# A two-block transformer kernel on one core: x also loaded by columns, bias rows from the host, another order at the start, and a shifted ring

## The chip, the core and the metric

The kernel runs on one core of a Trainium2 chip. A core has five engines that run their own instruction streams: TensorE (PE, matrix products), VectorE (DVE), ScalarE (ACT), GpSimd (POOL) and SyncE (SP), and 16 DMA engines that all queues share. SP and POOL issue the transfers here. The streams are tied together by semaphores alone: an instruction waits until a count is reached, another adds to it. The metric is the time of one execution on the device, in microseconds (us), median of the runs.

## What is computed

x has 256 rows (tokens) of 1024 numbers, all in 32-bit floats. The first block makes queries, keys and values of 24 heads in three groups with relative-position biases:

```
h = _rmsnorm(x, norm_gain[l])
z = h @ w_in[l]
a_in, a_gate, q, k, v, b_gp, g_logits = jnp.split(z, splits, axis=-1)
y_a = (_multiscale_pool(a_in, w_pool[l], pool_scale[l]) * jax.nn.silu(a_gate)) @ w_proj_a[l]
att = _dilated_attention(q.reshape(shp), k.reshape(shp), v.reshape(shp), rel_bias)
...
x = x + merged @ w_out[l]
```

where `_rmsnorm` is x times one root per row, times a gain per column. Because the root is one number per row, it can be applied behind the product as well: (x * gain) @ w, each row then times its root. The second block is a convolution mixer, an attention with a window (bias from `rel_bias_2`), and after each of them an expert layer with retrieval: each token picks 128 of 16,384 experts (8 heads, 16 each) and reads two rows of 1024 numbers of each:

```
u = jnp.take(u_tab, ic, axis=0)
h = jnp.einsum("cd,ced->ce", xc, u)
a = gc.astype(xc.dtype) * jax.nn.gelu(h, approximate=False)
return jnp.einsum("ce,ced->cd", a, jnp.take(v_tab, ic, axis=0))
```

## The kernel before

Everything is written out by hand in one function, one stream per engine; there is no scheduler, and the order in the code is the order on the engine. The tokens stand in two tiles of 128 (`TILES`), the 1024 columns in eight chunks of 128 (`KC`).

**The start.** SP issues x tile 0, the identity (part of `const`), x tile 1, `pf` (gains per column), the query weights of the first pair of heads in three parts by group (`first_landed`), the key weights, the table `bucket`, the rest of `const`, the value weights, `final_gain`, and then the weights of the further pairs as `wbuf` comes free (`load_heads`). TensorE does 16 products of ones with ones (L1008), turns the two tiles of x with the identity (16 transposes, `turn`, L959), does six more products of ones (L1015), and waits for ACT and DVE, which copy the turned chunks from PSUM, times the gain, to `raw` (`turned_out`, L698 and L1564). `raw` is x by columns with the gain and without the root. The first queries come of `raw` (`first_queries`, L1034). Meanwhile ACT sums the squares of each row (`norm`, L674) and DVE makes the roots of them (`root_of`) and a diagonal of them (`row_diag`, L1530); after the second group of queries TensorE spreads the roots over the partitions with two products (L1039). DVE copies them to `root_row`, makes `hT` = `raw` times roots (L1591), and scales the queries while it copies them to `q1` (L1594). Then it makes `hT4`, an arrangement of `hT` for the values (L1602, L1603).

TensorE goes on with `bias_rows`: four products of `rb` (the bias tables) with `bucket`, a table of zeros and ones (L1106 to L1110). ACT copies the result, POOL writes it to DRAM (L613, L614), waits for that, and reads it back in six loads with short strided rows, `hank0` (L618, twice) and `hank4` (L623, four times). DVE copies these reversed to `bias1` (L1608, L1611). The keys (`project`, L1025) come of `hT`, so TensorE waits for `hT_scaled` before them. ACT copies them to `k1` (L722). Then come the scores (L1061, L1067), the values (L1050), and the next pair of heads. There are four pairs (`PAIRS1`).

**The expert layers.** Two loops of 256 gathers. POOL issues one gather for each expert slot (L651, the last three of a layer in halves): 128 rows of 2048 numbers, 8 KB to each partition, into one of nine places of `ring`. DVE takes a dot product with the first half (L1906), ACT makes the weight and a diagonal of it (L834, L839, L844), TensorE adds the second half, weighted, in PSUM (L1373) and frees the place (`ring_free`). Between the products TensorE does those of later queries and keys. Their weights come to `wbuf` (L537) and to `w4`, a part of `arena` (L587, L590).

**Where things lie.** A tensor starts where the one before it ends, in the order of the `sb(...)` lines; `ring` is a part of `arena`:

```
sinks = sb("sinks", [P, HEADS2])
...
small = sb("small", [P, 64])
arena = sb("arena", [P, 32128])
...
ring = at(16, RING, 2 * D)
w4 = at(20640, KC, 512)
```

In the built program `arena` starts at byte 99,968 of each partition, so the first place of the ring at 100,032 (192 above a multiple of 512), and `w4` at 182,528, a multiple of 256; `wbuf` starts at 16,512, 128 above a multiple of 256.

Of the kernel before, what the change touches and what calls it, by code (L numbers as in the profile page):

```python
# [18 lines left out]
F32 = mybir.dt.float32  # L19
# [144 lines left out]
def bucket_table():  # L164
# [8 lines left out]
    rows.append(np.where(inside & (np.abs(rel) <= WINDOW2), buckets(-rel, 128), 32))  # L173
    return (np.arange(33)[:, None] == np.concatenate(rows)[None, :]).astype(np.float32)
# [14 lines left out]
def build(nc, A, out):  # L189

    with ExitStack() as ctx:
# [7 lines left out]
        bias_rows1 = nc.dram_tensor("bias_rows1", [HEADS1, ROWS1], F32)  # L199
        bias_rows2 = nc.dram_tensor("bias_rows2", [HEADS2, REL], F32)  # L200


# [9 lines left out]
        rb = sb("rb", [P, 24 + HEADS2])  # L212
# [5 lines left out]
        small = sb("small", [P, 64])  # L218
        arena = sb("arena", [P, 32128])
# [26 lines left out]
        bucket = at(16384, ROWS1 + REL)  # L246
        row1 = at(18432, ROWS1)
        row2 = at(19968, REL)
# [80 lines left out]
        rb_cleared = sem("rb_cleared")  # L329
        rb_loaded = sem("rb_loaded")  # L330
        pads_zero = sem("pads_zero")
        rows_done = sem("rows_done")
        rows_copied = sem("rows_copied")
        rows_stored = sem("rows_stored")
# [4 lines left out]
        roots_spread = sem("roots_spread")  # L339
        hT_scaled = sem("hT_scaled")  # L340
# [23 lines left out]
        k1_copied = sem("k1_copied")  # L364
        v1_copied = sem("v1_copied")
# [142 lines left out]
        def _(sp):  # L508
            sp.dma_start(x[:, 0], A["x"][0, 0:P]).then_inc(x_loaded[0], 16)
            sp.dma_start(const[:, C_ID:C_ID + P], A["const"][:, C_ID:C_ID + P]).then_inc(ident_loaded, 16)  # L510
            sp.dma_start(x[:, 1], A["x"][0, P:2 * P]).then_inc(x_loaded[1], 16)
            sp.dma_start(pf[:], A["pf"]).then_inc(param_loaded, 16)

# [4 lines left out]
            sp.wait_ge(chunk_done[0], ONE)  # L518
            for g in range(NG):
# [41 lines left out]
            sp.wait_ge(tile_turned, 4)  # L561
# [15 lines left out]
            sp.dma_start(bias2[1][:, :, 0:SEQ], bass.AP(bias_rows2, 0, [[1, P], [REL, HEADS2], [1, SEQ]])).then_inc(bias2_loaded[1], 16)  # L577
# [23 lines left out]
        def _(pool):  # L601
# [4 lines left out]
            nc.gpsimd.memset(rb[:], MASKED).then_inc(rb_cleared, 1)  # L606
            pool.wait_ge(rb_cleared, 1)
            pool.dma_start(rb[0:32, 0:24], A["rel_bias"]).then_inc(rb_loaded, 16)
            pool.dma_start(rb[0:32, 24:40], A["rel_bias_2"]).then_inc(rb_loaded, 16)
            pool.dma_start(sinks[:], A["attn_sink_2"][0].partition_broadcast(P)).then_inc(sinks_loaded, 16)  # L610

            pool.wait_ge(rows_copied, 2)
            pool.dma_start(bias_rows1.ap(), row1[0:HEADS1, :]).then_inc(rows_stored, 16)  # L613
            pool.dma_start(bias_rows2.ap(), row2[0:HEADS2]).then_inc(rows_stored, 16)  # L614
            pool.wait_ge(rows_stored, 32)
            for r in range(2):
                half = slice(r * CLASS, (r + 1) * CLASS)
                pool.dma_start(hank0[half], bass.AP(bias_rows1, r, [[CLASSES, CLASS], [ROWS1, HEADS1], [1, REACH]]))\  # L618
                    .then_inc(hank0_loaded, 16)
            for r in range(2):  # L620
                half = slice(r * CLASS, (r + 1) * CLASS)
                for j in range(2):
                    pool.dma_start(hank4[half, :, j], bass.AP(bias_rows1, REL + 2 * CLASS * (j ^ r),  # L623
# [1478 lines left out]
```

## Time and profile before

| | us |
|---|---|
| median of 3 runs | 1840.67 (1840.39 to 1841.07) |
| profiled execution | 1841.62 |
| its span, first to last instruction | 1839.8 |
| PE busy | 1611.0 (88%) |
| DVE busy | 1043.6 (57%) |
| ACT busy | 561.3 (31%) |
| POOL busy | 639.6 (35%) |
| DMA | 641.52 MB, mean 349 GB/s |

The busy shares are means over stages with different limits. In the page's slices of 46 us the DMA share stands at 9 tenths or more in slices 10 to 23 and 26 to 38, at about 421 GB/s; ahead of that it is lower and TensorE's is high. The numbers of a row are times from the span's start. A row of the chain of waits names what the end of the program hung on at that time, back from the last instruction. A product of 32-bit floats appears as two instructions in the trace, so x32 is 16 products. SP issues x tile 0 at 0.75 us, tile 1 at 1.66, the first query weights at 2.60, the third about 0.9 later, the key weights at 4.03; POOL issues the sinks at 2.95 and the six bias loads from 29.74 on. The first gather is issued at 420.33.

### The profile page before, as it was taken

What the parts mean: (1) busy time and instruction counts of PE and PEld (TensorE: products, weight loads), DVE (VectorE), ACT (ScalarE), POOL (GpSimd) and SP (SyncE); (2) the same over time, 40 slices, a digit from 0 to 9 for tenths busy, and PEclk for the clock granted to TensorE, in tenths of its full rate; (3) what the DMA queues carried; (4) which work ended last, traced back from release to release, by engine and by line L of the source; (5) the groups of instructions that cost most, each with busy time, mean ns of one, the idle gap of its engine ahead of it and who ended that gap; (6) DMA issues with size and microseconds to landing.
All of it is one profiled execution on the core that took longest, in us unless ns stands there. A gap on an engine that the chain in (4) does not pass through costs nothing.

```text
span 1839.8 us, 19448 instructions
## 1 busy us (share of the span) xinstructions
PE 1611.0 (88%) x6410; PEld 955.7 (52%) x6410; DVE 1043.6 (57%) x2669; ACT 561.3 (31%) x1711; POOL 639.6 (35%) x538
## 2 busy tenths in 40 slices
PE   9999999999989888888888789898987888877776
PEld 7888886887444444443444236644443444322222
DVE  4111202128667766666766654875676677666664
ACT  2111000102334333333333333433343333333332
POOL 1000000004444454343554530243444454455543
PEclk9999999999999999999999999999999999999999
DMA  8334337528999999999999986899999999999996
GB/s 259 135 112 163 113 138 278 214 92 320 422 421 421 421 421 421 422 422 421 421 421 415 418 332 229 365 421 422 421 420 422 421 421 421 421 421 416 412 416 275
DMA packets 87263, 641.52 MB, mean 349 GB/s; under 512 B 9715, under 2 KB 11907, under 8 KB 16380
## 3 DMA queue, kind: packets, MB, share of 16 engines
q0 software_dynamic: 75840, 540.92, 71.4%
q1 hardware_dynamic: 11324, 99.38, 14.1%
q8 instruction: 50, 0.82, 0.2%
q14 instruction: 49, 0.40, 0.1%
HBM read 639.15 MB, written 1.11 MB: 348 GB/s over the span
## 4 chain that ended last, share of the span: by engine, by line
PE 44%; DMA 39%; DVE 7%; ACT 5%; issue 5%; POOL 1%; DVEq 0%; SPq 0%; POOLq 0%; ACTq 0%
DMA arena<-in_peer_uv,arena 38%; PE ps L1373 15%; PE ps L1000 8%; DVE arena L1906 4%; PE ps L1025 4%; PE ps L986 3%; PE ps L1234 2%; PE ps L1050 2%; PE ps L975 2%; ACT arena L844 1%; PE ps L1305 1%; PE ps L1208 1%; ACT arena L839 1%; PE ps L1295 1%; PE ps L1200 1%
## 5 line engine op out<-in xcount | busy, mean ns | idle before, releaser
L1373 PE MATMUL ps<-arena 128*128 128x512 f32 x2048 | 951.3, 609 | 206.7 <-ACT arena L844 206.5
L651 POOL DMA_INDIRECT arena<-in_peer_uv,arena x506 | 614.9, 1215 | 979.0 <-PE ps L1373 545.2
L1906 DVE CUSTOM_DVE_ANT_0 arena<-xn,arena 128x1024 f32<-128x1024 f32 x512 | 627.2, 1226 | 385.6 <-DMA arena<-in_peer_uv,arena 376.7
L1373 PEld LDWEIGHTS ps<-arena 128*128 128x128 f32 x2048 | 376.3, 192 | 719.2 <-issue 387.8
L834 ACT ACTIVATE arena<-arena 128x2 f32<-128x2 f32 x252 | 51.3, 204 | 780.8 <-DVE arena L1906 780.6
L844 ACT ACTIVATE arena<-const,arena 128x128 f32<-128x128 f32 x504 | 174.7, 394 | 8.2
L839 ACT ACTIVATE arena<-arena 128x1 f32<-128x1 f32 x504 | 121.3, 288 | 8.2
L1000 PE MATMUL ps<-hT,wbuf 128*128 128x256 f32 x512 | 111.5, 379 | 0.0
L1234 PEld LDWEIGHTS ps<-hT,wbuf 128*128 128x128 f32 x768 | 92.9, 192 | 21.9 <-issue 21.0
L1000 PEld LDWEIGHTS ps<-hT,wbuf 128*128 128x128 f32 x512 | 97.0, 190 | 13.3 <-DVE arena L1679 0.2
L1234 PE MATMUL ps<-hT,wbuf 128*128 128x128 f32 x768 | 93.4, 275 | 0.6 <-ACT hT L698 0.6
L1025 PE MATMUL ps<-hT,wbuf 128*128 128x256 f32 x336 | 73.3, 379 | 0.0
L1627 DVE COPY arena<-ps 128x384 f32<-128x384 f32 x16 | 8.6, 555 | 109.5 <-PE ps L1076 108.6
L1025 PEld LDWEIGHTS ps<-hT,wbuf 128*128 128x128 f32 x336 | 63.5, 190 | 9.3 <-issue 0.9
L1842 DVE FIND_INDEX8 arena<-arena 128x8 uint32<-128x128 f32 (+1 forms) x184 | 59.0, 329 | 0.0
L986 PE MATMUL ps<-wbuf,arena 128*128 128x512 f32 x128 | 56.8, 593 | 0.3 <-DVE arena L1697 0.3
L1839 DVE MAX8 arena<-arena 128x8 f32<-128x128 f32 (+1 forms) x184 | 55.4, 329 | 0.3
L628 POOL DMA_DIRECT2D arena<-in_w_pool x1 | 0.8, 785 | 149.9 <-DVE arena L1634 149.9
L1695 DVE TENSOR_TENSOR arena<-ps,arena 128x1024 f32<-128x1024 f32 x2 | 2.5, 1225 | 76.9 <-PE ps L1000 76.9
L1050 PE MATMUL ps<-wbuf,arena 128*128 128x256 f32 (+1 forms) x256 | 43.0, 329 | 0.0
L1906 DVE DVE_READ_ACCUMULATOR2_ANT arena<- 128x1 f32 x512 | 42.3, 83 | 0.0
L1050 PEld LDWEIGHTS ps<-wbuf,arena 128*128 128x128 f32 x256 | 38.9, 191 | 3.6
(242 smaller groups left out, 1222.4 us busy)
## 6 DMA issues: line engine op xcount, KB each, us to landing
wbuf<-in_blocks SPq DMA_DIRECT2D x26, 2048.0 KB, 8.9
wbuf<-in_heads SPq DMA_DIRECT2D x11, 1536.0 KB, 7.1
arena<-in_blocks SPq DMA_DIRECT2D x7, 2048.0 KB, 12.3
arena<-in_peer_uv,arena POOLq DMA_INDIRECT x518, 15.0
arena<-in_subk SPq DMA_DIRECT2D x2, 1024.0 KB, 8.1
arena<-bias_rows POOLq DMA_DIRECT2D x1, 2048.0 KB, 10.7
arena<-bias_rows SPq DMA_DIRECT2D x1, 2048.0 KB, 18.6
wbuf<-in_heads SPq DMA_DIRECT2D x3, 512.0 KB, 8.2
```

Source lines behind the costliest of these rows:

```text
L651: pool.indirect_dma_start(to, None, A[f"peer_uv{layer}"], bass.IndirectOffsetOnAxis(ap=expert[:, unit % 2, e:e + 1], axis=0))\
L839: last = nc.scalar.activation(coef[:, b, e:e + 1], act_e[:, b, e:e + 1], ACT.Copy, scale=gate[:, b, e:e + 1])
L844: nc.scalar.activation(diag[:, place(unit, e)], ident, ACT.Copy, scale=coef[:, b, e:e + 1]).then_inc(diag_done, 1)
L986: last = mm(ps[t][:, j * 512:(j + 1) * 512], src[:, k, t * P:(t + 1) * P], wbuf[:, b, k], start=(k == 0), stop=(k == KC - 1), skip_group_c ...
L1000: last = mm(dst[:, m * SEQ:(m + 1) * SEQ], wbuf[:, b, k, m * P:(m + 1) * P], src[:, k - k0], start=(k == k0), stop=(k == k1 - 1))
L1025: last = mm(dst[:, g * SEQ:(g + 1) * SEQ], by_group(b)[:, g, k], hT[:, k], start=(k == 0), stop=(k == KC - 1))
L1050: last = mm(psB[:, t * 512 + cols_of.start:t * 512 + cols_of.stop], hT4[:, k, t, first:first + P], by_chunk(2)[:, k, cols_of], start=(k == ...
L1234: last = mm(to, w[:, k, col:col + P], hT[:, k, t * P:(t + 1) * P], start=(k == 0), stop=(k == KC - 1))
L1373: last = mm(ps[t][:, s * 512:(s + 1) * 512], diag[:, place(unit, e)], ring[:, place(unit, e), D + s * 512:D + (s + 1) * 512], start=(e == ...
L1839: last = nc.vector.max(value[:, eight], src)
L1842: last = nc.vector.max_index(index[:, eight], value[:, eight], src)
L1906: last = nc.vector.tensor_tensor_reduce(out=ring[:, place(unit, e), 0:D], in0=xn[:, v // PEER_HEADS], in1=ring[:, place(unit, e), 0:D], sc ...
```

## The change

The host now hands over two more inputs and two less. `xT` is x by columns in the layout of `raw`; `bias_rows1` and `bias_rows2` are the bias rows that TensorE made of table and bucket before. `bucket`, `rb`, `row1`, `row2` and the products, copies and DRAM writes that belong to them are gone. SP loads `xT` in two halves to `hT`; ACT scales the even chunks and DVE the odd ones to `raw`; TensorE no longer turns x. The first keys come of `raw` too, and DVE applies the roots in copying them. x is loaded by rows as well, later, for the sums of squares and as the residual. POOL waits for the second x tile before its first load. ACT does a small `Square` first, so that its table load stands ahead of all waits. A filler, `before_ring`, takes the place of `rb`: `arena` now starts at byte 100,288, and the places of the ring at multiples of 512. `w4` moves by the same 320 bytes.

```
-        rb = sb("rb", [P, 24 + HEADS2])
...
         small = sb("small", [P, 64])
+        sb("before_ring", [P, 120])
         arena = sb("arena", [P, 32128])
...
+            sp.dma_start(pf[:], A["pf"]).then_inc(param_loaded, 16)
+            load_columns(0)
+            load_first(0)
+            load_columns(1)
+            load_first(1)
+            sp.dma_start(const[:, C_ID:C_ID + P], A["const"][:, C_ID:C_ID + P]).then_inc(ident_loaded, 16)
+            for t in range(TILES):
+                sp.dma_start(x[:, t], A["x"][0, t * P:(t + 1) * P]).then_inc(x_loaded[t], 16)
+            load_first(2)
             load_heads(0, 1)
-            sp.dma_start(bucket[0:33], A["bucket"]).then_inc(const_loaded, 16)
+            load_heads(0, 2)
             sp.dma_start(const[:, C_INV:C_ALL], A["const"][:, C_INV:C_ALL]).then_inc(const_loaded, 16)
-            load_heads(0, 2)
...
+            pool.wait_ge(x_loaded[1], 16)
             pool.dma_start(sinks[:], A["attn_sink_2"][0].partition_broadcast(P)).then_inc(sinks_loaded, 16)
-
-            pool.wait_ge(rows_copied, 2)
-            pool.dma_start(bias_rows1.ap(), row1[0:HEADS1, :]).then_inc(rows_stored, 16)
-            pool.dma_start(bias_rows2.ap(), row2[0:HEADS2]).then_inc(rows_stored, 16)
-            pool.wait_ge(rows_stored, 32)
...
+            act.wait_ge(ones_ready, 1)
+            nc.scalar.activation(small[:, 62:63], ones[:, 0:1], ACT.Square)
             act.wait_ge(param_loaded, 16)
+            act.wait_ge(xT_loaded[0], 16)
+            for c in range(0, KC // 2, 2):
+                nc.scalar.activation(raw[:, c], hT[:, c], ACT.Copy, scale=pf[:, PF_NORM + c:PF_NORM + c + 1]).then_inc(raw_act, 1)
...
             for i in range(PAIRS1):
                 if i == 0:
                     first_queries()
-                    bias_rows()
-                    pe.wait_ge(hT_scaled, 1)
+                    project(psB, 1, 0, raw)
                 else:
+                    if i == 1:
+                        pe.wait_ge(hT_scaled, 1)
                     project(psA, 0, i)
...
+            dve.wait_ge(first_groups_done, 1)
+            scaled_out(k1, psB, range(NG - 1))
+            dve.wait_ge(chunk_done[1], ONE + 1)
+            scaled_out(k1, psB, (NG - 1,)).then_inc(k1_copied, 1)
             dve.wait_ge(hank0_loaded, 32)
```

In the new `first_queries` each of the first eight products waits for its chunk of `raw` (`raw_act`, `raw_dve`), and the two spreading products stand behind the third group of queries.

TensorE at the start, before (L1034 the first queries, L1039 the spreading, L1106 to L1110 the bias rows, L1025 the keys):

```order
L1008 MATMUL ps<-arena 128x128 x16
L959 MATMUL ps<-const,x 128x128 x16
L1015 MATMUL ps<-arena 128x128 x6
L1034 MATMUL ps<-arena,wbuf 128x256 x16
L1039 MATMUL ps<-arena 128x128 x2
L1034 MATMUL ps<-arena,wbuf 128x256 x8
L1106 MATMUL ps<-arena,rb 8x512
L1108 MATMUL ps<-arena,rb 8x128 x2
L1110 MATMUL ps<-arena,rb 16x512
L1025 MATMUL ps<-hT,wbuf 128x256 x24
```

and now (L1022 the first queries, L1027 the spreading, L1009 the keys, L1048 the first scores):

```order
L1003 MATMUL ps<-arena 128x128 x12
L1022 MATMUL ps<-arena,wbuf 128x256 x24
L1027 MATMUL ps<-arena 128x128 x2
L1009 MATMUL ps<-arena,wbuf 128x256 x24
L1048 MATMUL ps<-arena 128x256 x2
```

Between the products of ones and the queries nothing is left, and nothing between the spreading and the keys.

SP's transfers at the start, before (L520 the query weights, L516 the key and value weights):

```order
L509 DMA x<-in_x 128x1024
L510 DMA const<-in_const 128x128
L511 DMA x<-in_x 128x1024
L512 DMA pf<-in_pf 128x84
L520 DMA wbuf<-in_heads 128x1024 x3
L516 DMA wbuf<-in_heads 128x3072
L523 DMA arena<-in_bucket 33x1280
L524 DMA const<-in_const 128x1040
L516 DMA wbuf<-in_heads 128x3072
```

and now (L514 the query weights, L507 the key and value weights):

```order
L517 DMA pf<-in_pf 128x84
L511 DMA hT<-in_xT 128x1024
L514 DMA wbuf<-in_heads 128x1024
L511 DMA hT<-in_xT 128x1024
L514 DMA wbuf<-in_heads 128x1024
L522 DMA const<-in_const 128x128
L524 DMA x<-in_x 128x1024 x2
L514 DMA wbuf<-in_heads 128x1024
L507 DMA wbuf<-in_heads 128x3072 x2
```

Two halves of x by columns stand ahead, x by rows moved behind two of the query weights, and the third query weights and all that follow stand behind x.

DVE, from the roots' copy to the bias copies, before (L1594 the queries' copy, L1602 and L1603 `hT4`, L1608 the bias copies):

```order
L1590 COPY arena<-ps 128x256
L1591 TENSOR_TENSOR hT<-arena 128x2048
L1594 SCALAR_TENSOR_TENSOR arena<-ps,arena 128x256 x3
L1602 COPY arena<-hT 128x8x128
L1603 COPY arena<-hT 128x8x64
L1602 COPY arena<-hT 128x8x128
L1603 COPY arena<-hT 128x8x64
L1608 COPY arena<-arena 128x8x256 x2
```

and now (L1565 the queries' copy and, the second time, the keys'):

```order
L1574 COPY arena<-ps 128x256
L1575 TENSOR_TENSOR hT<-arena 128x2048
L1565 SCALAR_TENSOR_TENSOR arena<-ps,arena 128x256 x3
L1581 COPY arena<-hT 128x8x128
L1582 COPY arena<-hT 128x8x64
L1581 COPY arena<-hT 128x8x128
L1582 COPY arena<-hT 128x8x64
L1565 SCALAR_TENSOR_TENSOR arena<-ps,arena 128x256 x3
L1591 COPY arena<-arena 128x8x256 x2
```

The keys' copy came to DVE from ACT, and stands behind `hT4` and ahead of the bias copies.

## Rows read from the trace of the kernel before

**Rows 1.** Windows by stage: us, busy per engine (count), clock, DMA share, GB/s

```profile
60.00:460.00 400.00, 392.92 (x2275) 328.10 (x2274) 108.24 (x299) 49.77 (x123) 21.12 (x19) 1.00 0.46 175
...
456.00:1040.00 584.00, 501.43 (x1592) 251.85 (x1591) 393.55 (x976) 208.66 (x652) 270.93 (x224) 0.98 1.01 421
```

**Rows 2.** Chain of waits, first 70 us: start, length, what

```profile
10.18 7.14 PE ps L1034 x32
17.33 0.44 PE ps L1039 x4
...
21.23 0.95 PE ps L1106 x2
...
23.47 10.56 PE ps L1025 x48
34.03 0.95 issue
```

**Rows 3.** Issue to landing: x tiles (L509, L511); query weights (L520); key weights (L516); sinks

```profile
DMA to landing us min/median/max: 3.7/4.5/5.2
...
DMA to landing us min/median/max: 7.4/8.2/9.1
...
DMA to landing us min/median/max: 14.1/14.1/14.1
...
sinks<-in_attn_sink POOLq DMA_DIRECT2D x1, 8.0 KB, 7.2
```

**Rows 4.** Windows of the start, columns as in rows 1

```profile
5.00:10.00 5.00, 4.40 (x40) 4.20 (x38) 2.60 (x12) 3.36 (x11) 0.00 (x0) 1.00 0.98 283
10.00:15.00 5.00, 4.82 (x22) 4.29 (x23) 3.15 (x17) 0.51 (x2) 0.00 (x0) 1.00 1.02 408
...
31.00:41.00 10.00, 9.05 (x75) 7.16 (x74) 3.46 (x2) 0.81 (x1) 3.87 (x6) 1.00 1.02 213
```

**Rows 5.** Timeline of ACT and DVE at the start: start, length, engine, line, operation

```profile
7.29 2.18 ACT L698 ACTIVATE arena<-ps,pf 128x128 f32<-128x128 f32 x8 [1.64 <-DMA pf<-in_pf]
...
9.31 1.11 ACT L674 ACTIVATE xn<-x 128x1024 f32<-128x1024 f32 x1
...
11.48 0.15 DVE L1513 TENSOR_SCALAR meansq<-sumsq 128x1 f32<-128x1 f32 x1
...
13.38 0.29 DVE L1530 TENSOR_SCALAR arena<-const,rinv 128x128 f32<-128x128 f32 x1
...
21.26 1.64 DVE L1594 SCALAR_TENSOR_TENSOR arena<-ps,arena 128x256 f32<-128x256 f32 x3 [0.61 <-PE ps L1034]
...
25.37 0.62 DVE L1603 COPY arena<-hT 128x512 f32<-128x512 f32 x1
```

**Rows 6.** Landings of L516 issued at 34.1 and 47.8; POOL's queue, 0 to 14

```profile
DMA to landing us min/median/max: 11.7/11.7/11.7
...
DMA to landing us min/median/max: 6.2/6.2/6.2
...
q0 software_dynamic: 96, 0.01, 6.4%
```

**Rows 7.** Issue to landing in the loops: wbuf loads (480 to 870 us), L587, L590

```profile
DMA to landing us min/median/max: 11.4/11.6/12.0
...
DMA to landing us min/median/max: 11.3/11.3/11.3
...
DMA to landing us min/median/max: 12.3/12.3/12.3
```

**Rows 8.** SP's queue, 1184 to 1196 (w4), 525 to 538 (wbuf); two windows

```profile
q1 hardware_dynamic: 144, 2.10, 40.9%
...
q1 hardware_dynamic: 144, 2.10, 37.9%
...
302.00:314.00 12.00, 12.00 (x29) 5.32 (x28) 1.23 (x1) 0.88 (x1) 0.00 (x0) 1.00 0.99 426
...
640.00:740.00 100.00, 86.41 (x288) 43.77 (x287) 69.61 (x177) 34.22 (x109) 48.51 (x40) 1.00 1.01 421
```

More of the change, by code:

```diff
@@ L172, in bucket_table, with bias_rows @@
         rows.append(np.where((np.abs(apart) < SEQ) & (apart % dil == 0) & (np.abs(apart) <= window // 2), buckets(apart, 1024), 32))
-    rows.append(np.where(inside & (np.abs(rel) <= WINDOW2), buckets(-rel, 128), 32))
-    return (np.arange(33)[:, None] == np.concatenate(rows)[None, :]).astype(np.float32)
+    return rows, np.where(inside & (np.abs(rel) <= WINDOW2), buckets(-rel, 128), 32)
+def bias_rows(table, classes):
+    padded = np.concatenate([table, np.full((1, table.shape[1]), MASKED, np.float32)], axis=0)
+    return padded[classes].T
 def constants():
@@ L508, in _ @@
         def _(sp):
[L509 to L512, printed above, removed]
             def load_heads(i, b):
@@ L1006, in _, with project @@
             pe.wait_ge(ones_ready, 1)
-            for _ in range(16):
+            for _ in range(12):
                 mm(psD[:, 0:P], ones, ones, start=True, stop=True)
-            pe.wait_ge(ident_loaded, 16)
-            for t in range(TILES):
-                pe.wait_ge(x_loaded[t], 16)
-                turn(0, t, x)
-            for _ in range(6):
-                mm(psD[:, 0:P], ones, ones, start=True, stop=True)
-            for t in range(TILES):
-                turned_in(0, t)
-            def project(dst, b, i):
+            def project(dst, b, i, src=hT):
                 pe.wait_ge(w_landed[b], landed_value(b, i))
@@ L1033, in first_queries @@
                     for k in range(KC):
+                        if g == 0:
+                            pe.wait_ge(raw_dve if k % 2 else raw_act, k // 2 + 1)
                         last = mm(psA[:, g * SEQ:(g + 1) * SEQ], by_group(0)[:, g, k], raw[:, k],
                                   start=(k == 0), stop=(k == KC - 1))
-                    if g == 1:
-                        pe.wait_ge(xn_done, step(0, 1))
-                        for t in range(TILES):
-                            spread = mm(psD[:, 512 + t * P:512 + (t + 1) * P], ones, row_diag[:, t], start=True, stop=True)
-                        spread.then_inc(roots_spread, 1)
                 last.then_inc(chunk_done[0], 1)
+                pe.wait_ge(xn_done, step(0, 1))
+                for t in range(TILES):
+                    spread = mm(psD[:, 512 + t * P:512 + (t + 1) * P], ones, row_diag[:, t], start=True, stop=True)
+                spread.then_inc(roots_spread, 1)
             def project_values(i):
@@ L1585, in _, with scaled_out @@
                 norm(0, t, None, None)
-            dve.wait_ge(tile_turned_act, 2)
-            dve.wait_ge(tile_turned_dve, 2)
+            def scaled_out(to, src, groups):
+                for g in groups:
+                    last = nc.vector.scalar_tensor_tensor(out=to[:, g].rearrange("p (r a) -> p r a", r=CLASSES),
+                                                          in0=src[:, g * SEQ:(g + 1) * SEQ].rearrange("p (a r) -> p r a", r=CLASSES),
+                                                          scalar=HD ** -0.5 if to is q1 else 1.0, in1=root_row.rearrange("p (a r) -> p r a", r=CLASSES),
+                                                          op0=ALU.mult, op1=ALU.mult)
+                return last
+            dve.wait_ge(raw_act, KC // 2)
+            dve.wait_ge(raw_dve, KC // 2)
             dve.wait_ge(roots_spread, 1)
@@ L1592, in _ @@
             dve.wait_ge(chunk_done[0], ONE + 1)
-            for g in range(NG):
-                last = nc.vector.scalar_tensor_tensor(out=q1[:, g].rearrange("p (r a) -> p r a", r=CLASSES),
-                                                      in0=psA[:, g * SEQ:(g + 1) * SEQ].rearrange("p (a r) -> p r a", r=CLASSES),
-                                                      scalar=HD ** -0.5, in1=root_row.rearrange("p (a r) -> p r a", r=CLASSES),
-                                                      op0=ALU.mult, op1=ALU.mult)
-            last.then_inc(q1_copied, 1)
+            scaled_out(q1, psA, range(NG)).then_inc(q1_copied, 1)
             dve.wait_ge(hT_scaled, 1)
```

108 lines of the change are left out of this document (46 added, 62 removed).

## The prediction

> **What bounds the kernel now.** I read the windows by stage first. From 60 to 460 us TensorE is busy nearly without a break (393 of 400 us) while the DMA share is 0.46; from 456 us on the DMA share is 1.01 at 421 GB/s and TensorE has gaps (501 of 584 us) [rows 1]. So there are two regimes. Up to about 420 us, where the first gather stands, the time is TensorE's order of work, and whatever starts it earlier moves all that follows. Then come two loops of 256 gathers each, 1.05 MB a gather, limited by transfers: 512 x 1.0486 MB at 0.421 MB/us is 1275 us of the 1840. The second view is the chain of waits at the start [rows 2]: the query product runs from 10.18 to 21.23 (16 products, two spreading ones, 8 products), the small products for the bias rows from there to 23.47, the key product from 23.47 to 34.03, and after 0.95 us of "issue" the scores begin at 34.98. From there on TensorE stays busy [rows 1]. The third view is where transfers stand at the start: the x tiles land 3.7 and 5.2 us after their issue, the three query weights 7.4 to 9.1 after 2.6 to 3.5 (the first at 10.0), the first key weights 14.1 after 4.0 (so at 18.1) [rows 3]. The engines of the DMA are full from 5 us on, at only 283 GB/s from 5 to 10 and 408 from 10 to 15 [rows 4].
>
> The change touches both regimes: the first 35 us, and the address of the gathers' ring.
>
> **Part 1, TensorE's order at the start.** Removed are four warm-up products, 16 transposes, six dummy products, and the bias-row products. What matters is only when the key product begins, since after it the order is the same. I build that time up from landings.
> SP now issues pf (0.04 MB), half of the transposed x (0.52), query weights 0 (0.52), the other half (0.52), query weights 1 (0.52), the identity (0.07), x in two tiles (1.05), query weights 2 (0.52), key weights (1.57), value weights (1.57). The first x tile, 0.52 MB, landed at 0.75 + 3.7 = 4.45 [rows 3]; with pf ahead, the first half of xT lands at about 4.6. At the 283 GB/s of the window 5 to 10 the next ones follow at 6.5 (weights 0), 8.3 (second half), 10.1 (weights 1); then at 408: first x tile 11.6, second 12.9, weights 2 at 14.1, and the key weights 3.9 later, at 18.0, if nothing else runs.
> TensorE: chunks 0 to 3 wait for weights 0 (6.5; the scaling of the chunks, 2.18 / 8 = 0.27 us each for 128x128 on ACT [rows 5], say 0.4 for twice the columns, an estimate, two on each engine, is behind that landing). Chunks 4 to 7 wait for the second half plus scaling: 8.7 to 9.1. A 128x256 product costs 7.14 / 16 = 0.45 us [rows 2], so group 0 ends at about 10.8, group 1 (8 x 0.45 = 3.6) at 14.4, group 2 at 18.0, and the two spreading products (0.44) end at 18.4. They need both roots: the second x tile at 12.9 plus ACT's sum of squares (1.11, and 0.25 for reading it) and DVE's steps for one tile (11.48 to 13.67, 2.2 us) [rows 5], 16.5, so they don't wait. That a late query weight holds TensorE before 18.0 costs nothing more, unless it is over 14.1.
> **The key weights are late next.** GpSimd now waits for the second x tile and then issues the sinks and the six bias loads (hank0, hank4), 1.57 MB, right into this stretch. Before, the same six ran from 31 to 41, where the share is 1.02 at only 213 GB/s [rows 4]: 10 us of full DMA time for little data, since they are short strided rows. A weight load issued among them at 34.1 took 11.7 us against 6.2 for its like at 47.8 [rows 6]: 5.5 us lost. Now they come up behind a full SP queue. There GpSimd's small sinks load took 7.2 us to land [rows 3], so I put their data at 16 or 17 us, when the key weights are all but through: the sinks (6.4% of the engines' time of 14 us, 0.9 us [rows 6]) and half a microsecond of hank shared: 18.0 + 0.9 + 0.6 = 19.5. The ends: the fast end is no delay and faster early transfers, so that TensorE's own 17.7 decides; the slow end is a fair half share from 15 on, key weights at 21.7. I take 19.5, because the sinks row is the nearest to "GpSimd behind a full SP queue". **Key product: from 23.47 to 19.5, 4.0 us saved** (1.8 to 5.8).
> **After the key product** the copy of the keys is on DVE, two groups ahead and one behind the last product: one scalar_tensor_tensor of the three that took 1.64, so 0.55 [rows 5] and a tenth for the handover, in place of the 0.95 of the chain; 0.3 us saved. DVE must be through with the scaled hT, the queries and the hT4 copies: those ended at 25.99 with roots that were spread by 17.77 [rows 2, 5], 8.2 us; with roots at 18.4 that is 26.6, before the last group at 30. The bias copies follow the keys on DVE, as before, and TensorE wants the probabilities only two projections (2 x 10.56 us) later [rows 2]. The value weights end at 19 + 3.9 + shared time, about 27, wanted at 32. The 10 us of bias loads therefore cost only what they take from the key weights. If that cover is gone, the whole of it is the second rival below.
> The table load stays first on ACT, while transfers run: nothing. The bias rows no longer written to and read from DRAM: nothing beyond the 2.2 us already in the sum, and their loads were over by 41 [rows 4], behind TensorE's value product. TensorE's granted clock is 1.00, 2.4 GHz, in all the windows of the start [rows 4]; it now idles from about 5 to 6.5 and in part up to 8.7. Should the clock fall, 16 products at twice the time cost 3 to 4 us, of which the wait for the key weights (18.4 to 19.5) hides one.
> Sum of part 1: 4.0 + 0.3 = **4.3 us, from 1.1 to 6.1**. It arrives whole at the end, since nothing between 35 and 420 is tied to anything but TensorE's progress [rows 1, 2].
>
> **Part 2, the ring's address.** With rb and the new filler, ring place 0 moves from byte 100,032 to 100,352 of a partition as the built programs lay it out, that is from 192 above a multiple of 512 to 0; places are 8192 bytes apart, so all nine move alike. Does a destination's offset show? In the loops, w4 (an offset of 0 above a multiple of 256) and wbuf (128 above) are both loaded with 2 MB beside the gathers. w4 landed in 11.3 and 12.3 us, five wbuf loads in 11.4 to 12.0 [rows 7]: no difference. Finer, from the queue tables: w4's 144 packets took 40.9% of 16 x 12 us, 78.5; a wbuf load's 37.9% of 16 x 13, 78.8 [rows 8]. So 0.4% less, a little over the rounding of the shares (0.1 in 40 each). On 1275 us that is 0 to 5 us. The upper bound is what a stream without gathers reaches, 426 GB/s [rows 8]: 1275 x 5/426 = 15 us. A loss can't be excluded, but w4's worse landing (12.3) is the only row that hints at one; I allow 2 us. I take **2 us saved**, less than half of the 0.4%, since the landings show no difference at all.
> A page speaks for more. The Trainium skill, "DMA: Bandwidth & Descriptors", section "How a descriptor splits into AXI transactions", states that a transaction must start at a multiple of 256 bytes and that the bytes below an unaligned start still cost beats of 32 bytes. If it held for the destination, 192 bytes are 6 beats on 256, 2.3%, an estimate of 29 us over the loops. The rows of w4 and wbuf speak against it, and the page says it of bytes fetched.
>
> **Rivals.**
> (a) The address matters: the gathers rise from 421 to the 426 GB/s of the plain loads. 15 us on top of part 1: 1840.7 - 4.3 - 15 = 1821. For: the only streams above 421 have larger pieces or other offsets. Against: w4 against wbuf. By the rule of the Trainium skill's page above it would be more still, an estimate of 1807. Next bound: TensorE, busy 86 of 100 us in the loop [rows 8], so nothing stops it. 12%.
> (b) Slower: the bias loads get ahead of the key weights. As at 34.1, where a weight load stood behind them, the key weights wait for all of it: 14.1 + 3.9 + 0.9 + 9 = 27.9 in place of 23.5, so 4.4 us later, less 0.3: 1840.7 + 4.1 = 1844.8. It decides from a landing of the key weights later than 23.5 on. For: 213 GB/s at a full share. Against: the key weights are issued 8 us before the bias loads, and the sinks row. 6%.
> (c) The start is won and lost again: the early transfers are as slow as 283 GB/s because of x, pf and weights themselves and stay so up to the key weights, or the clock falls; the keys begin at 22 to 23. 1 us saved, and the address gives nothing: 1839.7. 14%.
>
> **How the numbers follow.** The profiled execution took 1841.62 (span 1839.8 and 1.8 around it), 0.95 above the median of 1840.67. Forecast: 1841.6 - 4.3 - 2.0 = 1835.3 by that execution, and **1834.4** by the median. 68%, with its own range of 1829.5 (6.1 and 5) to 1838.6 (2.1 and 0). Rival (a) is left below and (b) above; I take in (c): 1827.5 to 1839.7. A measurement of this kernel can tell about 0.2%, 3.7 us: faster means below 1837.0. The forecast's case is there with 9 in 10 of its weight, (a) wholly: 0.74 faster. Most of (c) and a tenth of the forecast: 0.19 within. (b) and a little of unknown causes: 0.07 slower.
>
> **What would show it.** In the chain of waits after, the key product begins at 19 to 20, released by the DMA of wbuf rather than by TensorE's own last product; the query product begins at 6 to 7 with a gap in group 0. The scores begin near 31 (34.98 before), and the first gather 4 us earlier than before. If the key product begins after 22, step 1 is wrong, and the DMA windows from 13 to 23 tell whether bias loads took the engines. Part 2 is right if the loop windows show 421 to 423 GB/s; at 426 or more rival (a) holds. If the start is 4 us earlier and the first gather isn't, the argument that TensorE alone carries the first 420 us is wrong.

## The result: 1818.04 us, some 16 us below the forecast

| | before | changed |
|---|---|---|
| median of 4 runs | 1840.76 (1840.39 to 1841.07) | 1818.04 (1817.82 to 1819.21) |
| profiled execution, its span | 1841.62, 1839.8 | 1817.82, 1815.8 |
| issue of the first gather | 420.33 | 415.58 |
| first loop, first to last issue | 663.17 | 652.38 |
| between the loops | 70.86 | 71.53 |
| second loop | 662.33 | 653.37 |
| from the last gather on | 23.09 | 22.92 |

The ratio is 0.9875, 95% interval 0.9862 to 0.9887. The lower five rows are start times of GpSimd's gather instructions in the two traces; together they are the 24.0 us between the spans. The start gave 4.8 us, the loops 10.8 and 9.0.

Windows of the changed kernel (us, busy per engine and count, clock, DMA share, GB/s), the ones that answer to [rows 1] and [rows 4]:

```profile
60.00:416.00 356.00, 351.15 (x2038) 296.54 (x2037) 73.18 (x197) 39.42 (x89) 2.15 (x3) 1.00 0.41 152
456.00:1030.00 574.00, 497.99 (x1571) 249.65 (x1570) 392.67 (x978) 207.46 (x649) 263.76 (x223) 0.98 1.01 426
5.00:10.00 5.00, 4.04 (x19) 3.31 (x18) 1.23 (x4) 1.81 (x4) 0.00 (x0) 1.00 1.02 402
```

and two within the loops, the first of which answers to the last row of [rows 8]:

```profile
640.00:740.00 100.00, 88.56 (x304) 46.03 (x304) 68.99 (x171) 35.05 (x112) 49.28 (x41) 1.00 1.01 428
1320.00:1420.00 100.00, 87.22 (x294) 44.40 (x293) 71.30 (x184) 39.58 (x122) 50.46 (x41) 1.00 1.01 427
```

The share was 1.01 before and is 1.01 now: the engines were just as full, and moved 421 GB/s before and 427 now. A full share says that an engine has a packet in hand, not that the packet takes as little time as it can. The packets of the two traces show what changed. From 640 to 740 us a gather's packet of 8 KB took 314.4 ns on average before, and only 7% of them took 309 ns; in the changed kernel 99.8% took exactly 309.

The chain of waits at the start (start, length, what), against [rows 2]:

```profile
5.46 13.31 DMA wbuf<-in_heads
...
18.82 10.64 PE ps L1009 x48
...
29.49 0.61 DVE arena L1565
...
30.23 0.70 PE ps L1048 x4
```

Issue to landing of the three query weights (L514, issued at 1.66, 2.60 and 4.91) and of the key and value weights (L507, issued at 5.46 and 6.0), against [rows 3]:

```profile
DMA to landing us min/median/max: 5.8/7.5/9.2
...
DMA to landing us min/median/max: 13.3/16.8/20.4
```

The key product begins at 18.82 where it began at 23.47, released by the DMA of its weights; the scores begin at 30.23 in place of 34.98. The first query weights land at 7.5, the key weights at 18.8 and the value weights at 26.4. DVE's timeline shows the keys' last group, and the bias copies waiting for the bias loads:

```profile
29.49 0.60 DVE L1565 SCALAR_TENSOR_TENSOR arena<-ps,arena 128x256 f32<-128x256 f32 x1 [2.24 <-PE ps L1009]
32.36 3.99 DVE L1591 COPY arena<-arena 128x2048 f32<-128x2048 f32 x2 [2.28 <-DMA arena<-in_bias_rows]
```

### The profile page after: what moved, and what is told of

Its sections match the earlier page's. It is cut to its first block, busy times and chain, and to the rows that moved or that the text cites. A ratio compares the mean times of both kernels' runs of the same rounds, so it can differ in the third digit from the quotient of the medians.

```text
span 1815.8 us, 19346 instructions
## 1 busy us (share of the span) xinstructions
PE 1606.2 (88%) x6366; PEld 953.2 (52%) x6366; DVE 1043.6 (57%) x2668; ACT 559.2 (31%) x1705; POOL 627.3 (35%) x533
## 4 chain that ended last, share of the span: by engine, by line
PE 43%; DMA 39%; DVE 7%; issue 5%; ACT 5%; POOL 1%; SPq 0%; DVEq 0%; POOLq 0%; ACTq 0%
DMA arena<-in_peer_uv,arena 37%; PE ps L1349 15%; PE ps L995 8%; DVE arena L1890 4%; PE ps L1009 4%; PE ps L981 3%; PE ps L1210 2%; PE ps L1037 2%; PE ps L970 2%; PE ps L1281 1%; ACT arena L839 1%; PE ps L1184 1%; ACT arena L834 1%; PE ps L1176 1%; PE ps L1271 1%
## 5 line engine op out<-in xcount | busy, mean ns | idle before, releaser
L646 POOL DMA_INDIRECT arena<-in_peer_uv,arena x506 | 605.5, 1197 | 969.6 <-PE ps L1349 554.2
L995 PE MATMUL ps<-hT,wbuf 128*128 128x256 f32 x512 | 111.5, 379 | 0.0
L1210 PEld LDWEIGHTS ps<-hT,wbuf 128*128 128x128 f32 x768 | 92.9, 192 | 21.9 <-issue 21.0
L995 PEld LDWEIGHTS ps<-hT,wbuf 128*128 128x128 f32 x512 | 97.0, 190 | 13.3 <-DVE arena L1663 0.2
L1009 PE MATMUL ps<-hT,wbuf 128*128 128x256 f32 x288 | 62.7, 379 | 0.0
L1009 PEld LDWEIGHTS ps<-hT,wbuf 128*128 128x128 f32 x288 | 54.5, 190 | 7.3
## 6 DMA issues: line engine op xcount, KB each, us to landing
arena<-in_bias_rows SPq DMA_DIRECT2D x1, 2048.0 KB, 18.8
```

The costliest lines, as they stand in the source:

```text
L646: pool.indirect_dma_start(to, None, A[f"peer_uv{layer}"], bass.IndirectOffsetOnAxis(ap=expert[:, unit % 2, e:e + 1], axis=0))\
L995: last = mm(dst[:, m * SEQ:(m + 1) * SEQ], wbuf[:, b, k, m * P:(m + 1) * P], src[:, k - k0], start=(k == k0), stop=(k == k1 - 1))
L1009: last = mm(dst[:, g * SEQ:(g + 1) * SEQ], by_group(b)[:, g, k], src[:, k], start=(k == 0), stop=(k == KC - 1))
L1210: last = mm(to, w[:, k, col:col + P], hT[:, k, t * P:(t + 1) * P], start=(k == 0), stop=(k == KC - 1))
```

## The experiments

**The two parts apart.** Theory: all that the loops won comes of the ring's address. The rival: it comes of the other order at the start, or of the data that are gone. First the address alone, in the kernel before:

```
         small = sb("small", [P, 64])
+        sb("before_ring", [P, 80])
         arena = sb("arena", [P, 32128])
```

> The kernel before with 320 bytes of filler ahead of arena and nothing else changed, so that the ring's places lie at multiples of 512. Theory A (the address sets the gathers' rate): the first gather stays at 420.3 us, the loop windows show 427 GB/s in place of 421, and the time is 22.7 less the 4.7 of the start, so 18 us less than before, about 1823. Theory B (the rate comes from something else in the new start or the inputs): 1841, 421 GB/s.

Measured: 1821.01 us (1820.51 to 1822.32), ratio 0.9885 (0.9868 to 0.9901). First gather at 420.38, as before; loops 653.5 and 652.8 us. The window of the first loop:

```profile
640.00:740.00 100.00, 87.66 (x300) 45.42 (x300) 71.86 (x185) 35.83 (x115) 49.27 (x41) 1.00 1.01 426
```

One line that computes nothing is worth 20 us. Then the changed kernel with its ring put back to 192 above a multiple of 512:

```
-        sb("before_ring", [P, 120])
+        sb("before_ring", [P, 40])
```

> The changed kernel with the filler cut to 160 bytes, so that arena and ring lie where they lay before (192 above a multiple of 512). Theory A: first gather at 415.6 as in the changed kernel, 421 GB/s in the loops, about 1836 us (4.7 less than before). Theory B: about 1818, 427 GB/s. If the two edits interact, e1 and e2 won't add up to 22.7.

Measured: 1837.76 (1836.8 to 1840.05), ratio 0.9979 (0.9969 to 0.9988). First gather at 414.63, loops 663.1 and 663.4:

```profile
640.00:740.00 100.00, 87.15 (x298) 44.76 (x297) 70.48 (x180) 35.30 (x114) 47.23 (x39) 1.00 1.01 421
```

The two parts add up: 0.9885 times 0.9979 is 0.9864, against 0.9875 for both at once, within the intervals. The start alone is worth about 3.5 us, the address about 20.

**Which addresses.** Bare gathers and loads, without the reference's computation: GpSimd issues 32 gathers of 8 KB to a partition for each of eight offsets, into six places, and no other engine reads them; then SP loads pieces of 7.5 KB with the destination or the source shifted.

> No part of the reference is computed: 8 stages of 32 gathers of 128 rows of 8 KB each, six places, no other engine at work, with the places at 0, 32, 64, 128, 192, 256, 448 and again 0 bytes above a multiple of 512; then 5 stages of 32 plain loads by SyncE of 128 rows of 7.5 KB, with destination and source offsets (0,0), (192,0), (0,192), (32,0), (0,0). Theory T1 (the address of the write alone costs time): stages at 0 run at 427 GB/s, at 192 at 421, also with nothing else going on; a boundary of 256 makes 256 as good as 0, a boundary of 512 doesn't. Theory T2 (it takes VectorE and TensorE reading the ring): all stages the same. The page's rule on the source: only the load stage with source offset 192 is slower, by about 2%. For plain loads with an unaligned destination I expect no loss, since loads of weights at 128 above 512 ran at their best.

The windows, in order: gathers with the places at 0, 32, 64, 128, 192, 256, 448 above a multiple of 512 and at 0 again; loads with (destination, source) at (0, 0), (192, 0), (0, 192), (32, 0), (0, 0). Columns: us, POOL busy, clock, DMA share, GB/s.

```profile
10.00:80.00 70.00, 24.41 (x27) 1.00 1.01 425
95.00:165.00 70.00, 23.46 (x26) 1.00 1.01 421
180.00:250.00 70.00, 23.40 (x25) 1.00 1.01 422
265.00:335.00 70.00, 23.41 (x25) 1.00 1.01 422
350.00:415.00 65.00, 22.53 (x25) 1.00 1.01 422
435.00:500.00 65.00, 22.47 (x24) 1.00 1.01 427
515.00:585.00 70.00, 24.67 (x27) 1.00 1.01 421
600.00:670.00 70.00, 24.20 (x26) 1.00 1.01 427
680.00:745.00 65.00, 0.00 (x0) 1.00 1.01 427
757.00:822.00 65.00, 0.00 (x0) 1.00 1.01 421
835.00:900.00 65.00, 0.00 (x0) 1.00 1.01 427
912.00:977.00 65.00, 0.00 (x0) 1.00 1.02 420
990.00:1050.00 60.00, 0.00 (x0) 1.00 1.01 427
```

So it needs neither readers nor gathers. (The first window, at 425, is of a stream that has just started; the repeat at 0 shows 427.) What counts is where the write starts: a multiple of 256 is free, 64, 128, 192 and 448 cost the same, 32 a little more. The source's address costs nothing: (0, 192) runs at 427. Does that carry over to the whole kernel? Places 256 above a multiple of 512, and no filler at all, which is 32 above a multiple of 64:

```
-        sb("before_ring", [P, 120])
+        sb("before_ring", [P, 56])
```

> The changed kernel with a filler of 56 numbers in place of 120, so that the ring's places lie 256 bytes above a multiple of 512; nothing else differs. Theory 256 (what costs is a write that does not start at a multiple of 256 bytes): loops at 427 GB/s, the first gather near 415.6, median 1818 +-1.5. Rival 512 (a multiple of 512 is needed, as the change's title says): loops at 421 to 422 GB/s, median 1836 to 1838. Rival bench (what the loads alone showed at this offset doesn't carry over to a loop in which VectorE, TensorE and ScalarE read the ring): anything between, 422 to 426 GB/s.

```
-        sb("before_ring", [P, 120])
```

> The changed kernel without any filler: rb is gone and nothing takes its place, so that the ring's places lie 32 bytes above a multiple of 64 but at no multiple of 256. This is what the change would have been without its thought for the address. Theory write (a write that starts off a multiple of 256 costs, and one at 32 a little more than one at 64, 128 or 192, as the bare gathers showed, 420.5 against 422.0 GB/s): loops of 664 to 667 us, median 1838 to 1843, so the start's 3.5 us are all but lost. Rival: the offset's size plays no part in a full loop, 1837.8 as with the ring at 192.

A window of the first:

```profile
640.00:740.00 100.00, 88.44 (x304) 45.91 (x304) 68.70 (x168) 34.57 (x111) 49.48 (x41) 1.00 1.01 427
```

and of the second:

```profile
640.00:740.00 100.00, 86.83 (x297) 45.07 (x298) 70.09 (x180) 35.22 (x113) 47.32 (x40) 1.00 1.01 420
```

256 gave 1817.45 (1816.87 to 1817.95), ratio 0.9872 (0.9855 to 0.9888): 256 is enough, and the multiple of 512 of the change is more than is needed. Without a filler it is 1841.45 (1840.66 to 1843.54), ratio 1.0005 (0.9995 to 1.0014). That is the kernel that someone writes who only improves the start: `rb` goes, all that lies behind it moves, and the start's gain is all but lost again, with nothing in the diff to show it. In the profiled execution the first gather is issued at 416.84, 3.5 us earlier than before (a lower clock at the start cost 1.6 us of the gain, see below), and the loops take 664.0 and 664.7 us, together 3.2 longer than before.

**How the charge grows with the piece.** The forecast had read 0.4% off two loads of 16 KB pieces. Plain loads again, by size of the piece; no reference is computed.

> No reference is computed and no engine but SP works. SP alone loads pieces of 16, 12, 8 and 4 KB per partition to places at a multiple of 512 and 192 bytes above one (16 KB also at 128), five places in turn. Question: in the kernel before, weight loads of 16 KB at offsets of 128 and 0 showed the same. Theory A (each piece pays once for its first partial transaction and once for its last, or not at all where the write is cut): the loss at 192 against 0 halves when the piece doubles: about 2.6% at 4 KB, 1.3% at 8 KB, 0.9% at 12 KB, 0.65% at 16 KB. Theory B (each transaction of the piece is shifted and pays): the same 1.3% at 4, 8, 12 and 16 KB. Theory C (16 KB pieces are cut otherwise and are free of it): 0% at 16 KB, 1.3% at 8 KB.

Windows in order (KB of the piece, offset): (16, 0), (16, 192), (16, 128), (12, 0), (12, 192), (8, 0), (8, 192), (4, 0), (4, 192):

```profile
33.00:61.00 28.00, 0.00 (x0) 1.00 1.01 432
114.00:142.00 28.00, 0.00 (x0) 1.00 1.01 428
195.00:223.00 28.00, 0.00 (x0) 1.00 1.00 427
269.00:290.00 21.00, 0.00 (x0) 1.00 1.01 430
331.00:352.00 21.00, 0.00 (x0) 1.00 1.01 426
385.00:437.00 52.00, 0.00 (x0) 1.00 1.01 427
465.00:519.00 54.00, 0.00 (x0) 1.00 1.01 422
540.00:586.00 46.00, 0.00 (x0) 1.00 1.03 420
604.00:651.00 47.00, 0.00 (x0) 1.00 1.03 410
```

The loss is 2.4% at 4 KB, 1.2% at 8 KB, 0.9% at 12 and 16 KB. The packets say it more finely: at a multiple of 512 nearly all took 159, 309, 460 and 611 ns, and in the windows at 192 they took 162.9, 313.8, 463.9 and 614.9 on average, so 3.9, 4.8, 3.9 and 3.9 ns more a piece. Theory A holds in its main point: the charge is one of some 4 to 5 ns for each piece, not a share of its bytes. Theories B and C fall.

The round windows leave out the beginning of each stage, and there the same writes cost nothing. Of the 16 KB stage at 192, which starts at 81.3, these are the windows ahead of 103 and behind 110; of the 12 KB stage at 192, which starts at 305.1, those ahead of 323 and behind 326:

```profile
84.00:103.00 19.00, 0.00 (x0) 1.00 1.01 432
110.00:157.00 47.00, 0.00 (x0) 1.00 1.01 429
...
308.00:323.00 15.00, 0.00 (x0) 1.00 1.01 430
326.00:352.00 26.00, 0.00 (x0) 1.00 1.00 425
```

Up to there the packets took 611 and 460 ns, as at a good place. The charge sets in 23 to 25 us after the start of a 16 KB stage, 19 after that of the 12 KB stage and 13 after that of the 8 KB stage. At all three sizes that is after some 35 to 39 pieces on each engine (at 4 KB, where the engines were not full at first, after 15 us).

> No reference is computed and no engine but SP works. Plain loads: 16 KB pieces at offsets 0 and 128 with five in flight and with two, 8 KB pieces at 0 and 192 with five and two, 2 KB pieces at 0 and 192 with five. Questions: why did 16 KB weight loads at 128 above a multiple of 256 run clean (611 ns a packet, 426 GB/s) in quiet stretches of the kernel before, and does the charge fall on the piece? Theory A (a charge per piece, for its cut first and last part): mean packet +3 to +5 ns at 8 and 16 KB whatever the number in flight, and at 2 KB as many ns, which is 4 to 6%. Theory B (it shows only when the write side is crowded by more than one load in flight): with two in flight no or half the charge. If 16 KB pieces at 128 are clean with two in flight, B is the reason for the quiet stretches.

Two 8 KB windows with two loads in flight, places at 0 and at 192, then 2 KB with five, at 0 and at 192:

```profile
508.00:582.00 74.00, 0.00 (x0) 1.00 0.82 304
615.00:688.00 73.00, 0.00 (x0) 1.00 0.85 311
707.00:750.00 43.00, 0.00 (x0) 1.00 0.97 322
762.00:804.00 42.00, 0.00 (x0) 1.00 0.95 318
```

With 16 KB pieces two in flight filled the engines as well as five, and the charge was the same (433 GB/s at 0 and 429 at 128 with five, 432 and 429 with two). With 8 KB pieces two in flight left the engines idle for part of the time (share 0.82 to 0.85), and the shifted place was no slower at all. There 309 ns was the time of 79% of the packets at a good place and of 77% at the shifted one. 2 KB pieces moved 1.2% less at 192, not the 4 to 6% less of theory A, and their packets show no charge: 84 ns for 94 and 92% of them. So the charge is one of a stream that fills the engines without a pause and has done so for a while, not a time that each piece takes by itself.

That also answers the expectation's first question. The 16 KB loads around 302 to 314 us in the kernel before wrote at 128 and 192 above a multiple of 512 and still took 611 ns a packet: their stretch had run for under 16 us, with 24 pieces of 16 KB on each engine, when it ended. In this run's 16 KB stages at 128 the charge sets in after 24 us as well, with five loads in flight and with two. The loops of the kernel before show it too: after slower traffic from 445 to 455 us (349 GB/s) nearly all gather packets of 455 to 461 took 309 ns, and of those of 465 to 500 only 9% did. What changes in that time, and why a single weight load at 128 or 64 above a multiple of 256 beside gathers at a good place took 611 ns in 95 to 100% of its packets, no run here shows.

**The start: do the bias loads hold the key weights?** GpSimd waits for the first key weights instead of the second x tile before it issues the sinks and the bias loads:

```
-            pool.wait_ge(x_loaded[1], 16)
+            pool.wait_ge(w_landed[1], 16)
```

> The changed kernel, with GpSimd's sinks and bias loads held until the key weights have landed. Theory of the forecast (they delayed the key weights): the key weights land near 17.6 in place of 18.8, the key product begins when the roots are spread, at 18.4, 0.4 us earlier. Rival (they come up too late to matter): key weights at 18.8 as before this edit. The price: hank4 lands later, and DVE's bias copies end after 41.9; if that matters, TensorE shows a gap before the first probabilities near 63.8; I expect none.

> The kernel of e3_bias_late again, timed: GpSimd waits for the first key weights instead of the second x tile before its sinks and bias loads. Theory: the bias loads hardly touch the critical path in the changed kernel (e3's key product began at 18.73, after the spreading, against 18.82), so 1817.5 to 1818.2, the same as the changed kernel. Rival: e3's single time of 1815.88 was real, and the gap between the loops (70.3 against 71.5 us) comes of it: 1816.0 to 1816.5, about 0.1% better than the changed kernel.

One profiled run: 1815.88 us, key product at 18.73, released by the spreading, first gather at 415.23. Timed: 1819.39 (1816.8 to 1823.14), key product at 18.18, first gather at 414.66. In the profiled one of these the first loop took 656.8 us, more than in any other kernel with a good place (652.3 to 653.8), and the runs spread over 6 us where the changed kernel's spread over 1.4. Whether this version is better is undecided; its interval (0.9861 to 0.9894) covers that of the changed kernel. At the key product the bias loads cost 0.1 to 0.6 us, about what the landings vary by themselves.

**The start: what the unscaled keys are worth.** The first keys come of `hT` again, and ScalarE copies them:

```
                     first_queries()
-                    project(psB, 1, 0, raw)
+                    pe.wait_ge(hT_scaled, 1)
+                    project(psB, 1, 0)
```

> The changed kernel, but the first keys come of hT (with the roots) as before, so TensorE waits for hT_scaled, and ScalarE copies them. Theory: in the changed kernel the spreading ends at 18.7 and hT is scaled 2.8 to 3.3 us later, so the key product begins at 21.3 to 22.0 instead of 18.8 and everything after it is 2.6 to 3.2 us later; first gather at 418.2 to 418.8, median 1820.5 to 1821.3. Rival (the keys' wait for their weights is the true limit, so the roots cost little more): key product at 19.0 to 19.5, under 1 us later, median 1818 to 1819.

Its chain of waits:

```profile
17.84 0.46 PE ps L1027 x4
...
18.88 2.30 DVE hT L1576
21.22 12.33 PE ps L1009 x48
33.58 0.82 ACT arena L717
...
34.53 0.70 PE ps L1048 x4
```

and its window from 22 to 31 us:

```profile
22.00:31.00 9.00, 9.00 (x35) 7.62 (x34) 3.76 (x6) 0.00 (x0) 0.00 (x0) 0.81 1.02 250
```

1821.53 us (1820.54 to 1825.4), 3.5 above the changed kernel and more than expected. The wait is the one that was expected (21.22 for 18.82, 2.4 us), but the product itself is 1.7 us longer, at a granted clock of 0.81 (0.50, the lower of its two levels, from 22.5 to 25.5): TensorE had stood idle from 18.30 to 21.22. Is it the idle time? The same kernel with 12 products of ones in the gap:

```
                     first_queries()
+                    for _ in range(12):
+                        mm(psD[:, 0:P], ones, ones, start=True, stop=True)
                     pe.wait_ge(hT_scaled, 1)
```

> The kernel of e8_keys_scaled with one addition: 12 products of ones with ones (128x128) between the spreading and the wait for hT_scaled, so that TensorE doesn't stand idle there. In e8 the key product ran 12.33 us against 10.38 in the changed kernel, at a granted clock of 0.81 from 22 to 31. Theory clock (TensorE's idle 2.9 us from 18.30 to 21.22 let its clock fall to 1.2 GHz for a while): clock 1.00 from 22 to 31, key product 10.4 to 10.6 long, scores at 32.6 to 33.0 and first gather near 418.0, median 1.7 to 2.0 us under e8's 1821.5, so about 1819.7. Rival contention (the key product was long because its weights or VectorE's writes of hT4 held it): it stays at 12.3, and the extra products only stand in its way; median 1821.5 or a little more.

```profile
21.52 10.64 PE ps L1009 x48
```

```profile
22.00:31.00 9.00, 9.00 (x44) 7.94 (x43) 4.10 (x6) 0.00 (x0) 0.00 (x0) 1.00 1.03 247
```

The clock stayed at 1.00 and the key product at 10.64 us, as long as in the changed kernel; contention is out. The scores began at 33.14 in place of 34.53, and the first gather at 418.48 in place of 419.89. The median doesn't show it: 1821.86 (1819.67 to 1822.5). In this execution the first loop took 653.8 us where e8's took 652.3, which is as much as the start had won. Read off the trace the clock costs 1.7 us, off the median nothing can be told.

The clock fell in one more execution, that of the kernel without a filler. Its chain of waits (L1021 is its query product), its timeline of TensorE ahead of it, and the window:

```profile
7.59 12.31 PE ps L1021 x48
```

```profile
7.59 0.70 PE L1021 MATMUL ps<-arena,wbuf 128*128 128x256 f32 x2 [1.82 <-DMA wbuf<-in_heads]
```

```profile
7.00:12.00 5.00, 4.41 (x13) 3.60 (x14) 0.62 (x2) 1.27 (x3) 0.00 (x0) 0.66 1.03 415
```

Here TensorE had waited 1.82 us, and the query product took 12.31 us instead of 10.7. In the seven other executions with the new start the same wait was 0.96 to 1.36 us, the clock stayed at 1.00, and the product took 10.7. The shortest of these waits is the changed kernel's:

```profile
7.51 0.70 PE L1022 MATMUL ps<-arena,wbuf 128*128 128x256 f32 x2 [0.96 <-DMA wbuf<-in_heads]
```

The Trainium skill, "TensorE: Matmul & The Clock Gate", section "Part 1: The HAM clock gate", says that the clock stands at 1.2 GHz when the array has been idle and at 2.4 once it has been busy. The two traces with a fall agree: it came behind waits of 2.9 and 1.8 us.

## Why the forecast was too high, step by step

**What bounds the kernel: right.** Two regimes, TensorE up to the first gather, transfers behind it. The scores came 4.75 us earlier and the first gather 4.76: the start's gain arrived whole, as said. In the loops TensorE was busy for 86 of 100 us and gave way to the faster stream (now 88.6).

**Part 1: right, 4.3 us forecast, 4.75 in the traces, 3.5 by the median of the ring at 192.** The key product was put at 19.5 and came at 18.82, released by its DMA as said. The landings that it was built from: first query weights 6.5, measured 7.5; the second and third 10.1 and 14.1, measured the same; the x tiles 11.6 and 12.9, measured 11.5 and 12.8; keys 18.0 before the bias loads and 19.5 with them, measured 18.8; value weights 27, measured 26.4. That the first came a microsecond late and the others didn't is two errors against each other, and so luck: a slower beginning, and 402 GB/s from 5 to 10 where the 283 of before was taken. The keys' copy on DVE cost 0.61 + 0.14 us in place of the 0.95 of [rows 2], 0.2 saved where 0.3 were put. That the unscaled keys matter was right, and by more than the wait: without them 2.4 us of waiting and 1.7 us of clock. Rival (c) didn't happen in the changed kernel, but its clock did in two of its relatives. It cost 1.6 to 1.7 us there, not the 3 to 4 that the forecast gave it. Rival (b) is out: the key weights landed 4.7 us before its point of 23.5. One slip of the sum changed nothing: its slow end, "from 1.1", is 1.8 + 0.3 = 2.1, which the range then used.

**Part 2: wrong, 2 us forecast, 19.75 measured between first and last gathers.** Rival (a), at 12%, was what happened, and even its 15 us were too few: the loops run at 427, not 426, and they last 1325.5 us, not the 1275 of the gathers' bytes alone (1325.5 x 6/427 = 18.6). Three steps failed.
- "w4 landed in 11.3 and 12.3 us, five wbuf loads in 11.4 to 12.0: no difference." Landings of a load that shares sixteen engines with gathers tell of the gathers' state more than of its own. All these loads stood beside gathers at a bad place. In the changed kernel's first loop wbuf lies where it lay, 128 above a multiple of 256, and 95 to 100% of its packets took 611 ns; before, beside the shifted gathers, 15 to 33% did, with means of 614 to 615. w4, at a multiple of 256 before, took 611 ns in 74 and 61% of its packets (means 612.0 and 612.5); now it lies 64 above one, and 98 to 99% take 611. The two did differ before, by 2 to 3 ns a packet, but neither of them paid anything once the gathers stood at a good place.
- "So 0.4% less. On 1275 us that is 0 to 5 us." The 0.4% was a true reading, from 16 KB pieces, and was carried over per byte. It is paid per piece. The same row gives 0.3 us over 128 pieces, 2.3 ns each; the loops have 512 x 128 pieces on 16 engines, 4096 on each, and that makes 10 us, with the rounding of the shares 3 to 16. The loops show 19.75 / 4096 = 4.8 ns, and 4.8 is also what the bare 8 KB stream shows.
- "I take 2 us, less than half of the 0.4%." This weighed the coarse row (landings, 1 us apart) against the fine one (shares), and let the coarse one halve the fine one.

The forecast also took 426 GB/s, the rate of a stream without gathers, as the most that the address could give. It was the row nearest to the truth, and stood as a rival only because of w4 against wbuf. But that it was clean was luck: its loads wrote at 128 and 192 above a multiple of 512 themselves, and showed the good rate only because their stretch was short. Read with their addresses, the row would have seemed to say that the address is free.

The page's rule, that a transaction starts at a multiple of 256 bytes (the Trainium skill, "DMA: Bandwidth & Descriptors", section "How a descriptor splits into AXI transactions"), names the right boundary: 256 is free, and 64, 128, 192 and 448 are not. Its size is another: 6 beats of 32 bytes on 256 would be 2.3%, an estimate of 29 us, where the loops show 1.5% (19.75 of 1325.5 us); the offsets 64, 128 and 192, which by beats below the start would cost 2, 4 and 6 of them, cost the same; and what it says of bytes fetched was not seen, since a source at 192 ran at 427 GB/s. Here the boundary counts on the side of the write.

## What to carry to other kernels

Where a loop is bound by transfers, look at the built address of what they write: in a long stream that keeps the engines full, every piece that starts off a multiple of 256 bytes in its partition cost some 4 to 5 ns here, 1.2 to 1.5% at 8 KB and 2.4% at 4 KB. A stretch of under 13 us, or single such loads among well placed ones, didn't show it, so don't conclude from those that the address is free. Any edit that adds or removes a buffer ahead of such a ring moves it, so compare the address before and after, and measure an edit of the start with the ring held in place. A difference read from pieces of one size is to be carried over per piece and per byte, and where the two disagree by a factor, that is the range.

## What the runs showed of the hardware

- A DMA share of 1.01 stood at 421, 427 and 432 GB/s alike, and 1.03 at 410 and at 420. The share can't tell a stream with shifted writes from one without; GB/s, or the time of one packet, can.
- Writes at 64, 128, 192 and 448 above a multiple of 512 all cost alike (421 to 422 GB/s against 427), 32 a little more (420 to 421), 256 nothing; sources cost nothing (427).
- The charge sets in late: the same 16 KB stream at 192 moved 432 GB/s in its first 20 us and 429 afterwards, and 8, 12 and 16 KB pieces all ran clean for some 35 to 39 pieces on each engine. Why is open.
- The charge is gone when the engines aren't full: 8 KB pieces with two loads in flight moved 304 GB/s at a good place and 311 at a bad one.
- A gap of 2.9 us in TensorE's work took its granted clock to 0.81 over the next 9 us and made a product of 10.6 us last 12.3; twelve products that compute nothing kept it at 1.00. A gap of 1.8 us ahead of the queries cost 1.6 us in another execution (clock 0.66 from 7 to 12); gaps of 1.0 to 1.4 us there, in seven executions, cost nothing. So an earlier start that makes TensorE wait once can lose 1.6 to 1.7 us more by the clock.
- Two executions of one kernel (the one with the late bias loads) took 652.3 and 656.8 us for the first loop, and the other five kernels with a good place 652.3 to 653.8, at the same rate in most of it. No run here says why, and it hides gains of 1 to 2 us at the start.
